# A hybrid decoder layer on one core: the opening's copies and sines reordered, the state and input rows loaded earlier, the output gates kept in another place

## The reference, cut to what matters

```python
def layer(x, states, w):
    h = rmsnorm(x, norm1_g)
    u, xr, gr, q, k, v, o, ig, fg = split(h @ w_in)      # 256,256,256,512,512,512,512,4,4
    # S5: complex diagonal recurrence, 16 groups x 64 states
    step = exp(log_step); mag = exp(lam_re * step)
    ab = mag * (cos(lam_im * step) + 1j * sin(lam_im * step))
    bb = ((ab - 1) / lam) * b                            # scaled input matrix
    s = scan(ab, bb @ u, s0); y5 = re(c @ s) + d * u
    y5 = gelu(y5) * sigmoid(gelu(y5) @ glu_w + glu_b)
    # Griffin RG-LRU: conv of 4 taps, gates r and i, a real recurrence
    xc = conv(xr, conv_state); r = sigmoid(xc @ wa + ba); i = sigmoid(xc @ wx + bx)
    hr = scan(exp(-8 * softplus(lam) * r), sqrt(1 - a * a) * i * xc, h0)
    yr = hr * gelu(gr)
    # mLSTM: 4 heads of 128, stabilised exponential gates
    p = (q @ k.T) * exp(gate differences - running max)
    ym = headnorm(p @ v / max(abs(row sums), exp(-m))) * sigmoid(o)
    x1 = x + concat(y5, yr, ym) @ w_out
    # mixture: top 4 of 32, clamped SwiGLU, 1024 -> 2 x 1024 -> 1024
    return x1 + moe(rmsnorm(x1, norm2_g))
```

## Time and profile before

| | |
|---|---|
| median of 3 runs | 1098.6 us (1098.29, 1098.60, 1100.36) |
| profiled execution | 1098.81 us |
| its span | 1097.0 us, 13183 instructions |
| busy: PE, PEld | 1036.5 us (94%), 435.2 us (40%) |
| busy: DVE, ACT, POOL | 316.1 us (29%), 197.9 us (18%), 95.3 us (9%) |
| read from HBM | 424.68 MB, 390 GB/s over the span |
| granted clock of TensorE | 0.993 |

### The profile page before, as it was taken

The page is one execution under the profiler, slowest core; times in us unless marked ns, Lnnn a source line. Parts: engine busy times, 40 slices in busy tenths (PEclk is TensorE's granted clock), DMA queues, the critical chain, the costliest instruction groups (busy, mean ns, idle before and its releaser), DMA issues.

```text
span 1097.0 us, 13183 instructions
## 1 busy us (share of the span) xinstructions
PE 1036.5 (94%) x5134; PEld 435.2 (40%) x5134; DVE 316.1 (29%) x640; ACT 197.9 (18%) x418; POOL 95.3 (9%) x177
## 2 busy tenths in 40 slices
PE   8999999999999999899889989999899989998997
PEld 5767745334333433343333323333324233433322
DVE  5889456312131212121202112121212121212023
ACT  5543615401110201011000201020102010100002
POOL 6899000000000000000000000000000000000000
PEclk9999999999999999999999999999999999999999
DMA  7533799999999999999999999999999999999995
GB/s 223 194 114 77 260 370 406 427 426 431 430 433 430 430 431 431 431 431 431 434 431 431 431 431 431 431 431 434 431 430 431 431 431 431 431 433 431 424 426 239
DMA packets 62051, 429.45 MB, mean 391 GB/s; under 512 B 12022, under 2 KB 25054, under 8 KB 33342
## 3 DMA queue, kind: packets, MB, share of 16 engines
q1 hardware_dynamic: 60868, 428.16, 93.5%
q10 hardware_dynamic: 1146, 0.79, 0.2%
HBM read 424.68 MB, written 3.67 MB: 390 GB/s over the span
## 4 chain that ended last, share of the span: by engine, by line
PE 55%; DMA 36%; DVE 5%; ACT 2%; issue 1%; SPq 1%; ACTq 0%; DVEq 0%
DMA ring_a<-in_exp_w_dram 27%; PE psum L2405 17%; PE psum L2440 14%; DMA ring_b<-in_exp_w_dram 8%; PE psum L2426 7%; PE psum L2327 3%; PE psum L2158 3%; PE psum L2350 2%; PE psum L1886 2%; PE psum L2449 1%; PE psum L2277 1%; PE psum L2283 1%; DVE rgb L1341 1%; SPq L449 1%; DMA xn<-in_x_prompt_dram 1%
## 5 line engine op out<-in xcount | busy, mean ns | idle before, releaser
L2405 PE MATMUL psum<-ring_a,xg 128*64 128x512 f32 x1200 | 341.8, 600 | 14.4 <-DMA ring_a<-in_exp_w_dram 14.4
L2440 PE MATMUL psum<-ring_a,aT 128*64 128x512 f32 x768 | 217.7, 596 | 8.5 <-DMA ring_a<-in_exp_w_dram 8.2
L2405 PEld LDWEIGHTS psum<-ring_a,xg 128*64 128x64 f32 x1200 | 102.9, 137 | 170.1 <-issue 166.0
L2405 PE MATMUL psum<-ring_b,xg 128*64 128x512 f32 x368 | 152.3, 598 | 7.8 <-DMA ring_a<-in_exp_w_dram 7.8
L1672 DVE TENSOR_TENSOR x<-x,psum 128x512 f32<-128x512 f32 x60 | 41.2, 687 | 367.7 <-PE psum L2350 367.7
L2426 PE MATMUL psum<-ring_a,xg 128*64 128x512 f32 x336 | 103.5, 608 | 14.2 <-DMA ring_b<-in_exp_w_dram 14.2
L2440 PEld LDWEIGHTS psum<-ring_a,aT 128*64 128x64 f32 x768 | 68.0, 137 | 110.2 <-issue 104.3
L2440 PE MATMUL psum<-ring_b,aT 128*64 128x512 f32 x256 | 104.0, 595 | 4.2 <-DMA ring_a<-in_exp_w_dram 2.6
L1760 DVE TENSOR_SCALAR acts<-psum 128x512 f32<-128x512 f32 x32 | 22.0, 688 | 223.3 <-PE psum L2426 207.8
L1045 ACT ACTIVATE acts<-acts 128x512 f32<-128x512 f32 x32 | 20.1, 627 | 296.5 <-DVE acts L1760 296.5
L2405 PEld LDWEIGHTS psum<-ring_b,xg 128*64 128x64 f32 x368 | 43.1, 136 | 75.5 <-issue 63.6
(11 more groups left out here) (508 smaller groups left out, 934.9 us busy)
## 6 DMA issues: line engine op xcount, KB each, us to landing
ring_a<-in_exp_w_dram SPq DMA_DIRECT2D x144, 2048.0 KB, 26.3
ring_b<-in_exp_w_dram SPq DMA_DIRECT2D x46, 2048.0 KB, 24.8
ring_a<-in_w_in_dram SPq DMA_DIRECT2D x4, 2048.0 KB, 8.5
ring_a<-in_w_out_dram SPq DMA_DIRECT2D x2, 2048.0 KB, 9.8
ring_a<-in_w_in_dram SPq DMA_DIRECT2D x3, 1024.0 KB, 5.9
ring_a<-in_state_ml_c_dram SPq DMA_DIRECT2D x4, 512.0 KB, 6.1
out_dram<-ring_a SPq DMA_DIRECT2D x4, 512.0 KB, 6.1
ring_b<-in_exp_w_dram SPq DMA_DIRECT2D x2, 1024.0 KB, 28.5
```

The lines of the kernel that those rows point to most:

```text
L2405: m = M(psum[64 * x:64 * x + 64, bk, :], xg[:, k, u, 64 * x:64 * x + 64], w[x][:, 512 * bk:512 * bk + 512], start=False, stop=(k == KD - 1))
L2440: m = M(psum[64 * x:64 * x + 64, 4 + nn, :], aT[:, 2 * j + s, 64 * x:64 * x + 64], w[x][:, 1024 * s + 512 * nn:1024 * s + 512 * nn + 512], ...
```

## The change

The change has six parts.

- Copies: DVE copies hT3 too (order 0, 2, 4, 3, 5), ACT only hT1; four filler products stand in place of two. PE waits for the copies of hT0, hT2 and hT4 before `u0`, and for the other three behind its fourth product (`rows_turned`).
- Sines: ACT waits for the argument of the magnitude alone (new semaphore `mag_arg`, from DVE L1252) before its Exp, Abs and Exp, and for `angle_reduced` only before the first Sin.
- State rows: their five loads stand ahead of the gate weights, b and c in SP's order, and `glw` behind w_in1; PE's transposes `par` stand in `xr0` behind its sixth product (`state_rows`). ACT copies u0, u1, gp, then the bias piece, then par.
- Places: `o_tok` lies in `stS`, and `o_out` waits for `e_ready` of all heads; `o2` and `squares` lie in `uT_rolled`.
- Reload: SP reloads x1 right behind expert step 7, after the last S5 scan and the moved biases, ahead of w_out's first half, and not behind step 1.
- `products` and `decays` stay where they were in x1.

```diff
--- before.py
+++ after.py
@@ -244,12 +244,13 @@
         gate_parts, part_sums = t_dve[:], sm[:, 18, :]
 
         rb = [x1[:].rearrange("p i n -> p (i n)"), 0]
-        o_tok, o2 = carve(rb, [128, 2, 512]), carve(rb, [128, 128])
+        o_tok = stS.rearrange("p h n -> p (h n)")[:, 0:1024].rearrange("p (i n) -> p i n", i=2)
+        o2, squares = uT_rolled[:, 0, 0:128], uT_rolled[:, 1, 0:128]
+        rb[1] = 9 * 128
         bias_in = carve(rb, [128, 768])
         bias_parts = carve(rb, [128, 3 * 384]).bitcast(BF16).rearrange("p (w n) -> p w n", w=3)
         rb[1] = 9 * 128
         products = carve(rb, [128, 2, T])
-        squares = products[:, 0, 0:128]
         rb[1] = 9 * 128 + 768
         decays = [t_dve[:], decay_1] + [carve(rb, [128, T]) for _ in range(4)]
 
@@ -468,6 +469,11 @@
             for c in range(6):
                 if c == 1:
 
+                    for x, name in enumerate(("state_s5_re", "state_s5_im")):
+                        sp.dma_start(srow[64 * x:64 * x + 64, :], a[name][0].rearrange("b (j g) p -> (b j) (g p)", g=2)).then_inc(sem("par_loaded"), 16)
+                    sp.dma_start(prow[0:32, :], a["state_ml_n"][0].rearrange("b h k -> (b h) k")).then_inc(sem("par_loaded"), 16)
+                    sp.dma_start(prow[32:48, :], a["state_rg_h"][0].rearrange("b (x n) -> (b x) n", x=2)).then_inc(sem("par_loaded"), 16)
+                    sp.dma_start(prow[48:96, :], a["state_rg_conv"][0].rearrange("b t (x n) -> (b t x) n", x=2)).then_inc(sem("par_loaded"), 16)
                     sp.wait_ge(sem("wgate_zero"), 1)
                     sp.dma_start(wgate[:, :, 0:2 * H], w_in_cols(GI0, 2 * H)).then_inc(sem("wgate_loaded"), 16)
                     for x, name in enumerate(("s5_b_re", "s5_b_im")):
@@ -476,15 +482,10 @@
                     for x, name in enumerate(("s5_c_re", "s5_c_im")):
                         for tt in range(2):
                             sp.dma_start(c_in[:, 2 * x + tt, :], a[name][0, 8 * tt:8 * tt + 8].rearrange("g c p -> (g c) p")).then_inc(sem("c_loaded"), 16)
-                    for x, name in enumerate(("state_s5_re", "state_s5_im")):
-                        sp.dma_start(srow[64 * x:64 * x + 64, :], a[name][0].rearrange("b (j g) p -> (b j) (g p)", g=2)).then_inc(sem("par_loaded"), 16)
-                    sp.dma_start(prow[0:32, :], a["state_ml_n"][0].rearrange("b h k -> (b h) k")).then_inc(sem("par_loaded"), 16)
-                    sp.dma_start(prow[32:48, :], a["state_rg_h"][0].rearrange("b (x n) -> (b x) n", x=2)).then_inc(sem("par_loaded"), 16)
-                    sp.dma_start(prow[48:96, :], a["state_rg_conv"][0].rearrange("b t (x n) -> (b t x) n", x=2)).then_inc(sem("par_loaded"), 16)
                     sp.dma_start(gb[:], spread(a["ml_gate_bias"][0:1, :], 0, 128)).then_inc(sem("gb_loaded"), 16)
                     sp.dma_start(m0[:], a["state_ml_m"][0].rearrange("b h -> h b")).then_inc(sem("gb_loaded"), 16)
+                if c == 2:
                     sp.dma_start(glw[:], a["s5_glu_w"][0].rearrange("(k p) n -> p k n", p=128)).then_inc(sem("glw_loaded"), 16)
-                if c == 2:
                     sp.wait_ge(*at("weights_zero", 1))
                     for x, name in enumerate(("rg_wa", "rg_wx")):
                         for n in range(8):
@@ -514,6 +515,10 @@
             sp.wait_ge(*at("s5_turned", J5))
             sp.wait_ge(*at("fin_ready", 1))
             load_step(0, 7, narrow=True, opening=True)
+            sp.wait_ge(*at("s5_scanned", J5))
+            sp.wait_ge(sem("bias_moved"), 16 * 12)
+            sp.dma_start(x1[:, 0:2, :], a["x_prompt"][0].rearrange("(i p) n -> p i n", p=128)).then_inc(sem("x1_loaded"), 16)
+            sp.dma_start(x1[0:TS, 2, :], a["x_sample"].rearrange("b t n -> (b t) n")).then_inc(sem("x1_loaded"), 16)
             sp.wait_ge(*fill_ended("ys1"))
             load_w_out(0)
             sp.dma_start(g2c[:, 0, :], a["norm2_g"][0].rearrange("(k p) -> p k", p=128)).then_inc(sem("g2_loaded"), 16)
@@ -522,11 +527,6 @@
             sp.wait_ge(*fill_ended("o2"))
             load_w_out(1)
             load_step(0, 1, narrow=True, opening=True)
-
-            sp.wait_ge(*fill_ended("yTs"))
-            sp.wait_ge(sem("bias_moved"), 16 * 12)
-            sp.dma_start(x1[:, 0:2, :], a["x_prompt"][0].rearrange("(i p) n -> p i n", p=128)).then_inc(sem("x1_loaded"), 16)
-            sp.dma_start(x1[0:TS, 2, :], a["x_sample"].rearrange("b t n -> (b t) n")).then_inc(sem("x1_loaded"), 16)
 
             sp.wait_ge(*at("s5_gelu", 2))
             sp.wait_ge(*at("y3_ready", H + 1))
@@ -736,21 +736,20 @@
             await_fill(act, "vec")
             A(vecs[:, 0:NVEC + J5], bank("vec")[:, 0:NVEC + J5], ACT.Copy).then_inc(drained[FILLS["vec"][0]], 1)
             act.wait_ge(drained[FILLS["vec"][0]], 1)
-            for i in range(2):
-                name = f"hT{2 * i + 1}"
-                await_fill(act, name)
-                for c in range(4):
-                    m = A(hT[:, 4 + c, 128 * i:128 * i + 128], bank(name)[:, 128 * c:128 * c + 128], ACT.Copy, scale=vec("norm1_g", 4 + c))
-                m.then_inc(drained[FILLS[name][0]], 1)
+            await_fill(act, "hT1")
+            for c in range(4):
+                m = A(hT[:, 4 + c, 0:128], bank("hT1")[:, 128 * c:128 * c + 128], ACT.Copy, scale=vec("norm1_g", 4 + c))
+            m.then_inc(drained[FILLS["hT1"][0]], 1)
             act.dma_start(bias_in[:, 0:512], a["exp_b1"][0].rearrange("e (q n) -> q e n", q=4)).then_inc(sem("bias_loaded"), 16)
             act.dma_start(bias_in[:, 512:768], a["exp_b2"][0].rearrange("e (q n) -> q e n", q=4)).then_inc(sem("bias_loaded"), 16)
 
             A(sm[:, 1, :], vecs[:, NVEC:NVEC + J5], ACT.Exp).then_inc(says_now("step_ready"), 1)
-            act.wait_ge(*at("angle_reduced", 1))
+            act.wait_ge(sem("mag_arg"), 1)
             A(sm[:, 5, :], sm[:, 2, :], ACT.Exp).then_inc(says_now("mag_ready"), 1)
             A(rsm[:, 0:2], vec("rg_lambda"), ACT.Abs).then_inc(says_now("act_rg"), 1)
             act.wait_ge(*at("act_rg", 1))
             A(g_exp[:, 12:14], rsm[:, 0:2], ACT.Exp, scale=-1.0).then_inc(says_now("act_rg"), 1)
+            act.wait_ge(*at("angle_reduced", 1))
             A(sm[:, 6, :], sm[:, 9, :], ACT.Sin).then_inc(says_now("angle_ready"), 1)
             A(sm[:, 7, :], sm[:, 8, :], ACT.Sin).then_inc(says_now("angle_ready"), 1)
 
@@ -771,10 +770,10 @@
                 copy_out(f"u{x}", uT[:, x, :], bank(f"u{x}")[:, 0:T])
 
             u_out(0)
+            u_out(1)
+            copy_out("gp", gate_parts, bank("gp")[:, 0:T])
             bias_piece(0)
-            u_out(1)
             copy_out("par", parT[:, 0:224], bank("par")[:, 0:224])
-            copy_out("gp", gate_parts, bank("gp")[:, 0:T])
 
             def xp_out(x):
                 await_fill(act, f"xr{x}")
@@ -865,6 +864,7 @@
 
             def o_out(name, i, c):
                 await_fill(act, name)
+                act.wait_ge(*at("e_ready", H))
                 A(o_tok[:, i, 256 * c:256 * c + 256], bank(name)[:, 0:256], ACT.Sigmoid).then_inc(drained[FILLS[name][0]], 1)
 
             await_fill(act, "rows")
@@ -1239,7 +1239,7 @@
                 says(TSC(xn[0:n, i, :], xn[0:n, i, :], nst[0:n, 4 + i:5 + i], None, ALU.mult), "xn_ready", i + 1)
             says(V.memset(v2[:, 128:129], 1.0), "ones_ready", 1)
             dve.wait_ge(drained[FILLS["vec"][0]], 1)
-            for k in (0, 2, 4, 5):
+            for k in (0, 2, 4, 3, 5):
                 i, hf = k // 2, k % 2
                 t0, n = TILES[i]
                 await_fill(dve, f"hT{k}")
@@ -1249,7 +1249,7 @@
 
             lr, li = vec("s5_lambda_re"), vec("s5_lambda_im")
             dve.wait_ge(*at("step_ready", 1))
-            dv(TT(sm[:, 2, :], lr, sm[:, 1, :], ALU.mult))
+            TT(sm[:, 2, :], lr, sm[:, 1, :], ALU.mult).then_inc(sem("mag_arg"), 1)
             dv(TT(sm[:, 3, :], li, sm[:, 1, :], ALU.mult))
             magic = 12582912.0
             dv(TSC(sm[:, 4, :], sm[:, 3, :], 1.0 / (2 * math.pi), None, ALU.mult))
@@ -1861,10 +1861,13 @@
                 turn_half(k)
                 if k == 3:
                     keep_warm(1)
-            keep_warm(2)
-            for k in range(6):
-                b, f = FILLS[f"hT{k}"]
-                pe.wait_ge(drained[b], f + 1)
+            keep_warm(4)
+
+            def rows_turned(hf):
+
+                for i in range(len(TILES)):
+                    b, f = FILLS[f"hT{2 * i + hf}"]
+                    pe.wait_ge(drained[b], f + 1)
 
             def channels(name, c, col, between=None):
 
@@ -1968,17 +1971,22 @@
                     if k == 2:
                         ends_fill(m, "grows")
 
+            def state_rows(k):
+
+                if k == 5:
+                    pe.wait_ge(sem("par_loaded"), 16 * 5)
+                    await_bank(pe, "par")
+                    TR(bank("par")[:, 0:128], srow[:], ident[:])
```

(11 more changed lines are left out.)

## The result

The median of 20 executions is 1107.99 us against 1099.01, ratio 1.0062 (95% interval 1.0050 to 1.0074; it is the ratio of the means, the medians lie 0.8% apart). The forecast was 1098.0 in a range of 1095.8 to 1100.4. The executions fall into two groups: 4 lie at 1098.2 to 1098.3, 16 at 1106.6 to 1109.3. The kernel before has such a second group too, but rarely: 3 of 91 executions of all comparisons lie above 1101.4 (1105.0 to 1106.5). The profiled execution is one of the 16: 1107.92, span 1106.2. So with the change a second, slower group, rare before, is the usual one. That the 3 of the kernel before take the same course as these 16 is not shown: no profile fell on one.

The account below looks back on a forecast made before the run. It took PE to bound the kernel up to 182.85 us and the expert weight stream later; -0.47 + 0.42 - 0.55 = -0.60 gave 1098.2 against the profiled run, 1098.0 against the median, range 1095.8 to 1100.4.

Parts of the forecast that it names:

- The local steps: In the opening: PE starts 0.33 us earlier, DVE resumes 1.69 earlier after the sine, L1313 starts 0.95 earlier.
- the near bound: Landing of the last b load behind the state loads: bounds 19.5 and 22.1 us, wanted by DVE at 19.75.
- Rival D: Opening: b lands 2.69 us later, so DVE is 0.75 later than before; about 1099.2, chance 0.12.
- rival A: Expert weight stream moves by the whole x1 reload, 2.75 us; about 1095.9, chance 0.09.
- What of this reaches the scans: From opening to S5 scans: they gain between 0.33 (PE) and 0.95 (DVE) us; 0.47 taken.
- The output gates: Sigmoid table load behind the added wait for e delays PE's kt2; bounds 0 and 0.42 us, 0.42 loss taken.
- rival E: Extra stop of about 1.4 us at the moved Sigmoid load, PE loses 1.80, not 0.42; 1099.4, chance 0.05.
- The reload: x1's 1.18 MB moved ahead of w_out0 lets the expert stream start earlier; bounds 0 and 1.5 us, 0.55 gain taken.
- C: x1's reload holds up w_out0 beyond its 7.8 us of slack, PE waits 4.6; about 1103, chance 0.07.
- The slower side: Chance 0.11 that the whole kernel gets slower, against 0.15 faster and 0.74 same.
- the sum: Whole kernel: -0.47 for the scans, +0.42 for the gates, -0.55 for the reload, -0.60 us in all.

Follow-up runs that it names:

- POOL held: Changed kernel with POOL's tables waiting for DVE's tenth product behind the sines (about 18.3 us); 11 executions at 1098.3 to 1100.2, median 1099.3, ratio 0.9999.
- all three remedies: Changed kernel with POOL's tables held to 18.3 us, its turns behind the e products and the Sigmoid table loaded early; median 1098.62, ratio 0.9997.
- sines late: Changed kernel with the sines alone undone (ACT waits for the reduced angle first again); 8 of 12 executions at 1098.4 to 1099.6, 4 at 1104.9 to 1105.5, ratio 1.0014.
- moved input: Changed kernel with the sines as before and PE's second S5 input behind k3's third product; 12 executions, 7 at 1098.5 to 1099.6, 5 at 1102.1 to 1104.1, ratio 1.0017.

## Why the prediction was wrong, point by point

- **The local steps held.** PE started at 12.75 (forecast 13.13; the input rows came 0.3 earlier in this execution), with the fillers ended before; DVE idled 0.47 for the sine, so the table load did go ahead of the wait; b was waited for 0.27, at the near bound; L1313 stood at 25.68 (forecast 25.95). Rival D did not happen. By their own terms two figures are slightly off, b wanted at 19.78 and not 19.75, rival A at 1095.8 and not 1095.9; nothing hangs on them.
- **The step that failed** is "What of this reaches the scans": between 0.33 and 0.95, 0.47 taken; the scans came 1.9 later than before. It carried a gain of DVE forward over 40 us with the durations of the profile before, as if these belonged to the instruction. They belong to its meetings with POOL, whose tables wait for the same sines and so moved too, by 2.1 at their start (16.19 for 18.27) against the 1.2 that DVE kept. POOL's work is named nowhere in the prediction: it was put at nothing without a reason. The step also took r's sigmoid as tied to PE's products, since its row has no idle time; a few instructions ahead of it stands ACT's wait of 1.16 for DVE's L1307, and by that wait the meeting at L1307 reaches r: 48.46 (forecast 47.3). Both bounds were gains. The changed durations could be read in the trace of before (0.96 and 1.76 at L1307 and L683), and the rule of the port stands in the section of the Trainium skill cited above.
- **The output gates**: 0.42 taken, 3.28 measured in the slow course, and 0.42 where the scans are in time (POOL held). The mechanism was right, the instruction order too; the size hung on e being ready at 106.99, which the failed step assumed. No drain behind the load was seen (114.06 + 1.28, then 115.35), so rival E was rightly small.
- **The reload**: 0.55 taken. Load 9 landed 8.9 us after its issue before, 9.5 with POOL held, 8.3 with all three remedies: nothing that can be told from noise, and rival A is out. No run has the reload alone, so whether it is worth 0.55 is not shown. w_out0 was in time, so C is out.
- **The slower side** was given 0.11 and one mechanism, the reload. It was another: a lock of two engines, for which no rival stood.
- Where the scans are in time, the sum is about right: 0.13 earlier at the first expert product with POOL held (forecast 0.05 there), 0.45 with all three remedies, where the early table takes the 0.42 of the gates out of the sum (forecast 0.47), and the 4 quick executions at 1098.2 to 1098.3 for 1098.0. This confirms no single term: the kernel before alone spreads over 2 us. That these 4 have the course of the run with POOL held is argued, not shown: no profile fell on one.

## What to carry to other kernels

A duration in a trace is not a property of an instruction where two engines share a port: before moving an engine in time, list which long instructions of the other it will then stand beside, and look in the rows for the same line at two durations. Two engines released by one semaphore meet in every round, and a round that is longer for it keeps them meeting; order them by a wait, as the turn behind the e product. And look at the executions one by one: a median over two groups says little, and even the kernel before has a second group (3 of 91), which the three executions known at the prediction did not show.

## What was not expected of the hardware

An idle time of PE does not by itself tell whether the clock falls: behind 1.74 us of it (sines late) the 16 products took 5.84 and the granted clock was 0.60 and 0.55 (76 to 78, 78 to 80 us), near the lower of its two levels, 1.2 GHz; behind 1.91 (moved input) it stayed at 1.00. A copy of three columns took 1.04 us for 0.20 where POOL's product had begun 0.03 before it. And 1.6 us of delay, once, cost 4.
